# An mLSTM, MoBA and NSA layer: value tiles and compressed scores moved into the last input projection, and a new order of work on GpSimd

## The reference

```
z = rms_norm(x) @ w_in                                  # 2964 columns: all inputs of the three groups
y_moba = block-sparse attention, 4 heads x 64           # own block of 256 keys causal + past block
y_ml   = mLSTM, 4 heads, qk 64, v 128, chunkwise        # num / max(|den|, exp(-m)), after silu(conv(q, k))
y_nsa  = g0 * compressed + g1 * selected + g2 * window  # 4 query heads x 64, gates g = sigmoid
y = [head_norm(y_moba), head_norm(y_ml) * sigmoid(lo), head_norm(y_nsa)]
x = x + rms_norm(y @ w_out)
x = x + rms_norm(relu(rms_norm(x) @ w1)^2 @ w2)         # hidden 4096
```

## Time and profile before

| | |
|---|---|
| median of 3 runs | 612.64 us |
| the profiled execution | 612.65 us |
| its span in the profile | 610.9 us |
| PE busy | 595.7 us (98%) |
| DVE, ACT, POOL busy | 390.0, 300.4, 256.1 us (64, 49, 42%) |
| chain that ended last | PE 92%, DVE 4% |
| share of DVE busy from 160 to 180 us | 18.75 of 20 us |

### The profile page before, as it was taken

One profiled execution on the slowest core, in us unless ns is written; L12 is line 12 of the kernel. 1 busy time (PEld: TensorE's weight loads), 2 busy tenths in 40 slices (PEclk: granted clock), 3 DMA queues, 4 the chain that ended last, 5 costly groups with the idle time before them and its releaser, 6 DMA issues.

```text
span 610.9 us, 8292 instructions
## 1 busy us (share of the span) xinstructions
PE 595.7 (98%) x3099; PEld 487.0 (80%) x3099; DVE 390.0 (64%) x665; ACT 300.4 (49%) x529; POOL 256.1 (42%) x137
## 2 busy tenths in 40 slices
PE   8999999999979999999999999999999999999995
PEld 5898888767756678889888888888888888888885
DVE  6414605355688883883899868577495695771657
ACT  7613424643758952564564625545445255453322
POOL 8553413644365430053159372533722725711611
PEclk9999999999989999999999999999999999999999
DMA  8743282383222530025225170440612503204002
GB/s 322 288 151 121 92 184 84 71 213 134 77 46 55 205 105 0 1 69 202 75 86 190 27 249 1 144 132 2 212 63 107 169 1 138 69 1 165 8 34 105
DMA packets 36580, 67.18 MB, mean 110 GB/s; under 512 B 2876, under 2 KB 23612, under 8 KB 35516
## 3 DMA queue, kind: packets, MB, share of 16 engines
q1 hardware_dynamic: 36236, 66.25, 33.5%
q10 hardware_dynamic: 304, 0.39, 0.3%
HBM read 62.18 MB, written 2.10 MB: 105 GB/s over the span
## 4 chain that ended last, share of the span: by engine, by line
PE 92%; DVE 4%; issue 1%; ACT 1%; DMA 1%; SPq 0%; POOLq 0%; POOL 0%; ACTq 0%; DVEq 0%
PE ps L1803 20%; PE ps L1805 20%; PE ps L1804 20%; PE ps L2265 7%; PE ps L2267 7%; PE ps L2266 7%; PE ps L2120 2%; PE ps L2135 2%; DVE stat L1451 1%; PE ps L2056 1%; PE ps L2025 1%; DMA x_land<-in_x_turned 1%; PE ps L1969 1%; PE ps L2057 1%; ACT probs L938 1%
## 5 line engine op out<-in xcount | busy, mean ns | idle before, releaser
L1803 PE MATMUL ps<-xT_h,ring_h 128*128 128x512 f32 (+1 forms) x384 | 144.2, 376 | 0.0
L1805 PE MATMUL ps<-xT_h,ring_l 128*128 128x512 f32 (+1 forms) x384 | 143.2, 373 | 0.0
L1804 PE MATMUL ps<-xT_l,ring_h 128*128 128x512 f32 (+1 forms) x384 | 143.0, 373 | 0.0
L765 POOL TENSOR_TENSOR ring_l<-raw_d,ring_h 128x1024 fp32r<-128x1024 f32 x25 | 67.4, 2700 | 129.8 <-ACT ring_h L1032 129.8
L765 POOL TENSOR_TENSOR ring_l<-raw,ring_h 128x1024 fp32r<-128x1024 f32 x31 | 76.7, 2502 | 77.5 <-DVE xres L1619 38.1
L689 POOL TENSOR_TENSOR ring_l<-raw,ring_h 128x512 fp32r<-128x512 f32 (+2 forms) x26 | 64.2, 2489 | 91.9 <-ACT ring_h L788 91.9
L1713 DVE TENSOR_TENSOR y<-ps,y 128x512 f32<-128x512 f32 x90 | 61.1, 688 | 51.0 <-PE ps L2267 50.7
L1803 PEld LDWEIGHTS ps<-xT_h,ring_h 128*128 128x128 f32 x384 | 72.4, 188 | 15.0 <-issue 2.4
L1805 PEld LDWEIGHTS ps<-xT_h,ring_l 128*128 128x128 f32 x384 | 72.3, 188 | 12.9
L1804 PEld LDWEIGHTS ps<-xT_l,ring_h 128*128 128x128 f32 x384 | 72.4, 188 | 12.6
L2265 PE MATMUL ps<-ring_h,a_h 128*128 128x512 f32 x196 | 76.7, 391 | 0.1
(11 more groups left out here) (277 smaller groups left out, 1002.8 us busy)
## 6 DMA issues: line engine op xcount, KB each, us to landing
raw<-in_w_mlp SPq DMA_DIRECT2D x16, 1024.0 KB, 5.5
raw_d<-in_w_mlp SPq DMA_DIRECT2D x16, 1024.0 KB, 6.2
raw<-in_w_groups SPq DMA_DIRECT2D x8, 1024.0 KB, 4.8
xres<-in_x SPq DMA_DIRECT2D x8, 512.0 KB, 6.4
raw<-in_nsa_cmp_w SPq DMA_DIRECT2D x8, 512.0 KB, 6.5
raw<-in_w_groups SPq DMA_DIRECT2D x8, 256.0 KB, 5.3
raw<-in_w_out SPq DMA_DIRECT2D x2, 1024.0 KB, 5.2
raw<-in_w_out SPq DMA_DIRECT2D x4, 512.0 KB, 4.4
```

Of the source, the lines that this page charges most:

```text
L765: nc.gpsimd.tensor_tensor(slot(ring_l, n), slot_source(n), slot(ring_h, n).bitcast(F32), ALU.subtract).then_inc(lo_done, 1)
L1803: nc.tensor.matmul(o, sh, mh, start=start, stop=False)
L1804: nc.tensor.matmul(o, sh, ml, start=False, stop=False)
L1805: return nc.tensor.matmul(o, sl, mh, start=False, stop=stop)
```

## The change

- Into the last projection: `half_feature(J_MK[1], ...)` gets `values_and_scores` in place of `alone`. Ahead of step k it issues: k = 1 value tiles 0 and 1; k = 2 tiles 2 and 3; k = 3 the compressed keys and values and tiles 4 and 5; k = 4 tiles 6 and 7; k = 5 scores 0 and 1; k = 6 the compressed scores. Behind the projection stand scores 2 and 3 and the first transposes, and then PE waits until the key eviction has freed bank 0, where score 4 goes now.
- ACT evicts the value tiles ahead of the first exponentials. The high half of w_out's chunk C_WO + 1 moves from the start of the attention into unit 11.
- DVE does the mLSTM sums and divisors ahead of the key eviction `mk_evict(1)`, and the roots in units 0 to 3 where it was 3 and 4.
- POOL: the gating comes ahead of all eight MoBA low halves (before, four stood ahead of it), and the low half of chunk C_WO + 1 comes after all eight (before, ahead of all).
- ACT writes the MoBA high parts in units 3 to 10 where it was 1 to 4 and 7 to 10.

```diff
-S_BANK = [2, 3, 0, 1, 7]
+S_BANK = [2, 3, 7, 1, 0]
-MB_UNITS = [1, 2, 3, 4, 7, 8, 9, 10]
+MB_UNITS = [3, 4, 5, 6, 7, 8, 9, 10]
...
@@ gpsimd
             low_half(C_WO)
-            low_half(C_WO + 1)
-            for n in range(HEADS):
-                moba_low(n)
             pool.wait_ge(ml_rn, 1)
             for t in range(NT):
...
                 nc.gpsimd.tensor_tensor(yml, yml, hid[:, t, :, 0:DV], ALU.mult).then_inc(ml_y, 1)
-            for n in range(HEADS, 2 * HEADS):
+            for n in range(2 * HEADS):
                 moba_low(n)
+            low_half(C_WO + 1)
             low_half(C_WO + 2)
             low_half(C_WO + 3)
@@ scalar
+            ml_evict(0)
+            ml_evict(1)
             act.wait_ge(kv_cmp, 2)
...
             last.then_inc(kc_ready, 1)
-            high_half(C_WO + 1)
+            ml_evict(2)
+            ml_evict(3)
             exp(0)
             exp(1)
-            ml_evict(0)
-            exp(2)
-            ml_evict(1)
-            ml_evict(2)
             act.wait_ge(cs_sub, 1)
             nc.scalar.activation(cexp[:], cexp[:], ACT.Exp).then_inc(cs_exp, 1)
-            ml_evict(3)
+            exp(2)
...
+                if u == 11:
+                    high_half(C_WO + 1)
                 if u in (15, 19):
                     high_half(C_WO + 2 + (u == 19))
@@ vector
             gelu_rest()
-            mk_evict(1)
+            ml_sums(0)
+            ml_sums(1)
             cmp_values()
+            ml_sums(2)
+            ml_sums(3)
             row_max(0)
             row_max(1)
-            ml_sums(0)
+            ml_divisors()
+            cmp_max()
+            mk_evict(1)
             row_max(2)
-            ml_sums(1)
-            cmp_max()
...
                 if u == 0:
-                    ml_sums(2)
-                    ml_sums(3)
+                    rsqrt_seed(SS_ML, R_ML, DV)
+                    link(rsqrt_step(R_ML))
...
                 if u == 2:
-                    ml_divisors()
+                    link(rsqrt_step(R_ML))
                 if u == 3:
-                    rsqrt_seed(SS_ML, R_ML, DV)
-                    link(rsqrt_step(R_ML))
-                if u == 4:
-                    link(rsqrt_step(R_ML))
                     link(rsqrt_step(R_ML))
                     rn = stat[:, R_ML:R_ML + 16]
@@ tensor
+            def values_and_scores(k):
+
+                if k == 1:
+                    pe.wait_ge(*reads(J_ST + 1))
+                    ml_values(0)
+                    ml_values(1)
+                if k == 2:
+                    ml_values(2)
+                    ml_values(3)
+                if k == 3:
+                    cmp_keys_values()
+                    ml_values(4)
+                    ml_values(5)
+                if k == 4:
+                    ml_values(6)
+                    ml_values(7)
+                if k == 5:
+                    score(0)
+                    score(1)
+                if k == 6:
+                    cmp_scores()
...
-            half_feature(J_MK[1], C_MK, 1, alone)
+            half_feature(J_MK[1], C_MK, 1, values_and_scores)
...
-                if s == 0:
-                    pe.wait_ge(ml_used, 3)
...
+            pe.wait_ge(ml_used, 4)
+            score(2)
+            transposes(0)
+            pe.wait_ge(cs_sub, 1)
+            score(3)
+            pe.wait_ge(*reads(J_MK[1]))
             for u in range(NU):
                 g, i = divmod(u, NT)
                 for m in range(2):
                     s = 2 * u + m
-                    if s == 0:
-                        transposes(0)
-                        pe.wait_ge(ml_used, 4)
                     if s + 4 < 2 * NU:
                         score(s + 4)
```

More of the change, by code:

```diff
@@ L2059, in score @@
                                  stop=True, skip_group_check=True).then_inc(s_done, 1)
-            pe.wait_ge(gelu_ready, 1)
-            for t in range(2):
[L2063 to L2092, removed]
@@ L2093, in _, with cmp_keys_values @@
-            score(3)
+            def cmp_keys_values():
+                pe.wait_ge(gelu_ready, 1)
+                for t in range(2):
+                    last = nc.tensor.matmul(ps[:, KV_BANK, 0:NP_], w2k[:, t].rearrange("p s d -> p (s d)"), gel[:, t, 0:NP_],
+                                            start=(t == 0), stop=(t == 1))
+                last.then_inc(kv_cmp, 1)
+                for t in range(2):
+                    last = nc.tensor.matmul(ps[:, KV_BANK, DH:2 * DH], gelr[:, t].rearrange("p h n -> p (h n)"), w2v[:, t, :],
+                                            start=(t == 0), stop=(t == 1))
+                last.then_inc(kv_cmp, 1)
@@ new lines, in cmp_scores @@
+            def cmp_scores():
+                pe.wait_ge(kc_ready, 1)
+                pe.wait_ge(vc_ready, 1)
+                nc.tensor.matmul(ps[:, KV_BANK, :], identb[:], mask_c[:, :, 0:1, :].to_broadcast([P, NT, HEADS, NP_]), start=True, stop=True)
+                for i in range(NT):
+                    for p in range(2):
+                        c = (HEADS * i + 2 * p) * NP_
+                        last = nc.tensor.matmul(ps[:, KV_BANK, c:c + 2 * NP_], nqT[:, p, i * P:(i + 1) * P],
+                                                kc2[:].rearrange("p m n -> p (m n)"), start=False, stop=True, skip_group_check=True)
+                last.then_inc(cs_done, 1)
@@ new lines, in _ @@
+            half_feature(J_MQ[0], C_MQ, 0, first_spreads)
+            half_feature(J_MQ[1], C_MQ, 1, other_spreads)
+            pe.wait_ge(silu_done, 4)
+            key_transposes(0)
+            key_transposes(1)
+            near_scores(0)
+            near_scores(1)
+            half_feature(J_MK[0], C_MK, 0, quarters)
+            states(0)
+            states(1)
+            bank_free(J_HT)
+            pe.wait_ge(*reads(J_H))
+            pe.wait_ge(fold_ready, 1)
+            pe.wait_ge(small_in, 16 * 3)
@@ L2095, in cmp_transposes @@
+            for t in range(2):
+                for j in range(2):
+                    n0 = NP_ * (2 * t + j)
+                    last = nc.tensor.matmul(ps[:, JOB_BANK[J_HT], n0:n0 + NP_], hsb[:, j, t * P:(t + 1) * P], fold[:],
+                                            start=True, stop=True)
+            last.then_inc(job_done, 1)
+            half_feature(J_MK[1], C_MK, 1, values_and_scores)
             def cmp_transposes():
```

## The result

The changed kernel takes 623.76 us (median of 4 runs, 622.89 to 624.3), the kernel before 612.59 beside it: ratio 1.0179, 95% interval 1.0161 to 1.0196, slower by 11 us. The profiled execution is the run of 622.89, its span 621.1 us for 610.9.

A forecast was written before the change was run, and what follows sets the result against it. PE was taken as the bound, busy 98%, with at best 7.8 us of waits and slow clock to win. Profiled 612.65 + 7.4 (score 32 later) + 1.7 (clock) - 0.5 = 621.25, stated as 621.0; range 615.5 to 625.5.

The forecast's parts named there:

- The step on which it rested: SP's queue: C_WO + 3's load waits for POOL's late low half, holding the MoBA copies; score 32 7.4 us later.
- six blocks in the projection: PE, last projection: each block laid between steps costs 0.21 us; bounds 0 and 1.3 us, 1.2 taken.
- end of POOL's chain: POOL from 171.6: gating 9.5, eight low halves 10.8, low half 5.0 us, ending at 196.9, later than ACT's chain at 195.9.
- from there to score 32: SP and DMA: issue of the load and pair 0's copies, landing behind 1 MB; 7.9 us taken, score 32 at 204.8.
- slow clock: PE after its wait of some 12 us: lower clock level, costing 0 to some 3.5 us, 1.7 taken.
- given back later: Behind score 32: small waits after 197 us (0.8 us) partly go, -0.5 us; nothing else later gives back.
- the signs that the prediction names: Profile after: PE wait of 9 to 14 us, load issued at 196 to 199, clock near 0.5 for 3 to 4 us.
- rival 3: Loop: POOL and DVE hold one another up and the slow clock lasts twice as long, 1.8 + 1.7 us; 624.5, chance 0.11.
- The early gain: First units of the attention loop: less waiting for DVE; PE at tile 28's score at 187.5 instead of 191.91, 4.4 us ahead.
- collisions: DVE ahead of `ml_rn`: long operations held up beside POOL's would no longer be, 2.1 us won.
- Rival 1: SP's queue: copies land by 193, before PE needs them, so the early gain stays; 608.2 or 610 us, chance 0.07.
- Rival 4: Projection: a block waits inside, PE wins nothing early, `ml_rn` 2 us later; 623 us, no chance of its own.

The follow-up runs named there:

- copies_first: The changed kernel with SP's load of chunk C_WO + 3 behind the twelve MoBA copies instead of ahead of them; 608.73 us and, run again, 608.9 us.
- pair0_ahead: The changed kernel, but SP, after the same wait, issues pair 0's six copies ahead of the load of C_WO + 3; 618.43 us, ratio 1.0083.
- pair1_late: The changed kernel, but SP issues pair 1's copies and all behind them only once score 32 is made; 623.42 us in one run.
- The four kernels: The kernel before, and three with late C_WO + 1 and C_WO + 3 load last: POOL's gating ahead (0.9967), projection blocks (0.9928), both (0.9942).
- pool_only: The kernel before with only POOL's new order, ACT's late high half and the new units for MoBA high parts; 626.05 us, ratio 1.0222.

## Why the prediction was right

Forecast 621.0 us (615.5 to 625.5), slower; measured 623.8, the profiled execution 622.9, the fastest of its four. The step on which it rested, the load of C_WO + 3 ahead of the copies in SP's queue, is shown by copies_first; pair0_ahead splits what follows it into waiting and queueing. By its own terms, against the profile after (its positions are 0.54 us early against the forecast's, by the head start named above):

| term | forecast | measured |
|---|---|---|
| six blocks in the projection | +1.2 us | about 0 |
| score 4 starts | 161.0 | 159.38 |
| `ml_rn` | 171.5 | 170.1 |
| score of tile 28 | 187.5 | 187.12 |
| gating, eight low halves, low half | 9.5 + 10.8 + 5.0 | 9.1 + 11.6 + 5.0 |
| end of POOL's chain | 196.9 | 195.8 |
| from there to score 32 | 7.9 | 9.6 |
| score 32 | 204.8 | 205.40 |
| slow clock | 1.7 | 2.15 |
| given back later | -0.5 | -0.06 + 0.15 |

The total is nearer than the terms are. With the head start taken out, POOL's chain ended 0.5 us sooner than forecast, and then all went the other way: 1.7 us from there to the score, 0.45 of slow clock, 0.6 not given back. Score 32 is 8.50 us later where 7.4 was forecast. Going from 621.25 down to 621.0 because the terms were "rather taken long" was a step in the wrong direction. Of the signs that the prediction names, two were off: the load was issued from 195.84, just before the 196 to 199 forecast, and the clock was low for 5.1 us, not 3 to 4.

- **The blocks** were mis-sized. From the projection's first step to score 4 it is 17.51 us (141.87 to 159.38) with a wait of 0.2 for the key eviction; before it was 17.40. The timeline of PE in the changed kernel shows why:

```profile
142.42 0.40 PE L1803 MATMUL ps<-xT_h,ring_l 128*128 128x512 f32 x1
142.65 1.05 PE L1997 MATMUL ps<-lv,W 128*128 128x129 f32 x8
...
144.06 0.50 PE L1801 MATMUL ps<-xT_h,ring_h 128*128 128x512 f32 x1
144.40 0.40 PE L1802 MATMUL ps<-xT_l,ring_h 128*128 128x512 f32 x1
```

A block of value tiles starts 0.23 us behind the step ahead of it, the plain distance, where the compress block of rows 3 took 0.33. Only the way back costs (0.34 for 0.23), and blocks among themselves had paid something of the kind in the bridge already: scores 0 and 1 were 0.37 us apart there and are 0.27 in the projection. The nearest row was not near enough, and the lower bound, nothing, was right.
- **POOL's chain** binds, as forecast: ACT's high half is done at 190.3, POOL comes to it at 190.88. The eight low halves took 0.8 us more, operations being held up beside DVE (3.06 us for two instead of 2.64, and one of 1.61): rival 3's mechanism at 0.8 us where I had put 1.8. The gating itself was not held up. On DVE's side the forecast of about 1 us each "as it did before" read the rows before too evenly: the gates of `coefficients` took 0.93 us there and 0.17 now, the first sum of `attn_out` 0.82 there and 1.62 now.
- **From POOL to the score** the byte terms were right (6.6 us; 6.8 in pair1_late). What was missing lies behind the last byte, where I had put nothing: in pair1_late, with nothing else on the engines, the last byte is gone by about 204.2 and the score starts at 205.57, 1.4 us later. Ahead of the first byte I had enough (1.5 us forecast; 9.4 - 6.8 - 1.4 = 1.2 there, gaps included). The prediction put the copies behind the chunk by the rule of the Trainium skill (DMA: Bandwidth & Descriptors, Queues, rings and completion order) that on each DMA engine the descriptors of one issuer are taken in ring order. pair0_ahead agrees: a copy lands 2.9 us sooner once the chunk is no longer ahead of it.
- **The clock**: a longer slow stretch, as in rival 3: 5.1 us at 0.5 instead of 3.4, though it cost 0.45 us more than the 1.7 of the earlier trace rows and not 1.7 more.
- **Given back**: the small waits behind unit 20 stayed (0.20 and 0.34 us in both profiles).
- **The early gain** came in size (tile 28's score 4.25 us sooner, counted from the projection's first step; forecast 4.4) but not by the sum as written; that its size was right is in part luck. I added 3.4 us of moved sums and divisors and 2.1 us of collisions as if each were worth its length. The four kernels say otherwise: either half takes away most of the same stall. Tile 28's score comes 3.4 us sooner by POOL's order, 4.6 by the bridge, 4.3 by both, and the whole is 1.9, 4.3 and 3.4 us faster. The terms overlap. Whether POOL's order costs something once DVE's sums are elsewhere, the intervals don't settle.

Rival 1 (the copies in time) was off by its condition, as argued; copies_first is what it looks like when that condition is met, 608.7 and 608.9 us for its 608.2. Rival 4 (nothing won early) was off too, since `ml_rn` came at 170.1. Its later `ml_rn` is what pool_only has, though that kernel does win early (tile 28's score 3.4 us sooner): the gating starts 3.0 us later there than in the changed kernel, score 32 3.2 us later, and the ratio is 1.0222 for 1.0179, 2.6 us more; I had put 2.

## What to carry to other kernels

Before moving a piece of work on one engine, list the transfers that wait for it and everything queued behind them in the same queue: here a low half that PE reads only in the output projection, 36 us or more after it is made, held twelve copies, and PE stood waiting for them before it was made (from 193.22, the low half ended at 195.83). When work moves later, let what waits for it move down the queue too. And before two cures for one stall are put in together, try each alone: their gains may not add; here 1.9 and 4.3 us made 3.4.

## What the runs showed of the hardware

- The time at the lower clock after a rest of PE doesn't follow the rest's length. After waits of 2.3, 8.3, 12.2 and 15.0 us the clock stayed low for 3.4 (kernel before), 2.9 (pair0_ahead), 5.1 (changed kernel) and 4.1 us (pool_only) of work. The penalty, by the length of tiles 32 to 40 against 8.52 us, was 1.1 (9.59), 2.15 (10.67) and 1.7 us (10.19); for the wait of 2.3 us it is half of the 3.4, worked out and not measured. Products whose result nobody reads, 11.4 us of them, kept the clock at 1.00.
- Copies of 128 KB issued on one queue are delayed by what is ahead of them (4.8 to 5.5 us to landing behind 1 MB, 2.4 ahead of it) and hardly, in one run, by what is behind them (12.0 us of wait in pair1_late, where nothing was issued behind pair 0 before score 32, and 12.2 in the changed kernel, where pair 1's six copies, 0.79 MB, were).
- DVE and POOL hold one another up: a sum of two SBUF operands on DVE took 1.45 to 1.69 us beside POOL's block and 0.69 to 0.77 elsewhere, and a POOL operation beside DVE 1.61 for 1.28.
